# An eighth V slot in the gather ring of a streaming encoder, with the space for it taken from three work buffers

## The chip, the core and the metric

The kernel runs on one core of a Trainium2 chip: TensorE (PE) multiplies matrices, VectorE (DVE), ScalarE (ACT) and GpSimd (POOL) work beside it, and SyncE (SP) issues plain transfers. Sixteen DMA engines carry all transfers of the core between HBM and the on-chip memory. The metric is the device time of the whole kernel in microseconds (us).

## What is computed

One step of an encoder layer for 1024 prompt rows and 32 sample rows of width 1024: an input projection, an mLSTM and a sliding-window attention on its halves, an output projection, and then PEER, a layer that fetches single experts by index. PEER does most of the work here. Cut to what matters:

```
def block(xb):                                    # peer, 128 rows at a time
    q = (xb @ w_q).reshape(TB, PEER_HEADS, PEER_KEY_DIM)
    s1 = jnp.einsum('thd,nd->thn', q[..., :PEER_HALF], sub_keys_1)
    s2 = jnp.einsum('thd,nd->thn', q[..., PEER_HALF:], sub_keys_2)
    t1, i1 = lax.top_k(s1, PEER_TOPK)
    t2, i2 = lax.top_k(s2, PEER_TOPK)
    cand = (t1[..., :, None] + t2[..., None, :]).reshape(...)
    cidx = (i1[..., :, None] * N_KEYS + i2[..., None, :]).reshape(...)
    top, sel = lax.top_k(cand, PEER_TOPK)
    idx = jnp.take_along_axis(cidx, sel, axis=-1)
    g = jax.nn.softmax(top.astype(jnp.float32), axis=-1)
    u = jnp.take(expert_u, idx, axis=0)
    a = jax.nn.gelu(jnp.einsum('thkd,td->thk', u, xb), approximate=False)
    ve = jnp.take(expert_v, idx, axis=0)
    return jnp.einsum('thk,thkd->td', g * a, ve)
```

There are 8 heads with 16 picks each, so every row fetches 128 rows of `peer_u` and 128 of `peer_v`, 4 KB each. At the end each row is normalised once more (`rmsnorm(x, norm_final_w)`).

## The kernel before

**Tiles and groups.** The rows are cut into 9 tiles of up to 128 rows. For PEER, 32 rows of a tile times 4 heads fill the 128 partitions: that is a group. Two groups (a pair) cover the 8 heads of 32 rows; there are 66 groups. A group has 16 steps, one for each pick. In a step one U tile (128 rows of `peer_u`) and one V tile (128 rows of `peer_v`), each 512 KB, are gathered with an indirect DMA.

**The ring.** The gathers land in `ring`, which has `NU` = 5 slots for U and `NV` = 7 for V. GpSimd issues all gathers in one fixed order, U of the next group and V of this one in turn (lines 583 and 594). Before a U gather it waits until VectorE has finished with the slot (`u_free`), before a V gather until TensorE has (`v_free`, line 590). The first V gathers wait for nothing, except that slots 5 and 6 hold staging pieces (`po`) of the first projection, whose stores must have ended (`proj_out`, line 593).

**A step on each engine.** VectorE multiplies the U tile with the spread rows `h2p` and sums (line 1255), giving one dot product for each partition. ScalarE turns a group's dots into gelu weights (line 822). VectorE makes the weight matrices `wk` of a group from them (`weigh`, line 1210). TensorE multiplies the V tile with its weight matrix into `acc` (line 1651). VectorE is one group ahead of TensorE. At the end of a pair TensorE moves the right half, which stands in other partitions, over: ScalarE copies it to `part` (`gather_parts`, line 833) and TensorE brings it back (line 1606). TensorE also spreads the rows of the next pair into `h2p` (`spread_rows`, line 1597), once VectorE has its last dot of the pair; VectorE waits for that before the next pair.

**Top-k.** VectorE picks the 16 experts of a group three groups ahead, in 11 stages (`topk`), one stage behind each of the steps 0 to 10. Stages 8 and 9 turn the flat position of each pick into two key indices: the position's high and low four bits are compared with 0 to 15 (a one-hot row, line 1190), multiplied with the key indices `i2f` (line 1193) and summed (line 1195). Stage 10 writes `idx`, from which GpSimd gathers. Both indices are done side by side in `co`, whose first half is also `cand`, the candidates.

**All else** is laid between the steps by tables of step numbers (`PE_AT`, `ACT_AT`, `DVE_AT` with `slot_of`): the projections, mLSTM, attention, queries and key scores of the next tiles. Each engine runs its own list in the order written. In attention four matrix products with `ident` write the window mask `wmask` into the scores (line 1481) before the keys are added. At a tile's end ScalarE takes the squares of the finished rows into `part` (`square_rows`, line 844).

## Time and profile before

| | before |
|---|---|
| median of 3 runs | 3442.43 us (3436.01 to 3443.79) |
| the profiled execution | 3454.89 us |
| its span, first to last instruction | 3453.2 us |
| mean granted TensorE clock | 0.810 of full speed |
| busy: TensorE / VectorE / GpSimd / ScalarE | 76% / 61% / 58% / 16% |
| gathers (software queue) | 1107.43 MB of 1197.01 MB in all |

Busy shares are means over the whole kernel. A row of the waits view says which engine, at which tile and line, stood idle until what, with the total, the number of times and the longest. In the timeline a row gives start, duration, engine, line and operation, how many instructions were merged, and in brackets the idle time of the engine before it and what ended it. "issue" means that nothing in the profile explains the gap, and "remote" that the releaser could not be named.

### The profile page before, as it was taken

Reading aid. Unit: us, or ns where it says so; the run is one execution under the profiler, and the core shown is the slowest. Engines: PE = TensorE matmul, PEld = TensorE weight load, DVE = VectorE, ACT = ScalarE, POOL = GpSimd, SP = SyncE. Lnnn points to the kernel's source line nnn. Section 1 sums busy time; section 2 is a strip of 40 time slices with the busy share of each in tenths; the row PEclk is TensorE's granted clock in tenths of the full one; section 3 lists DMA queues with packets and bytes.
Section 4 is the critical chain, followed back from the end, with each engine's and each line's share of the span. In section 5 each row is a group of like instructions: output and inputs, shape, how many; then the busy total and the mean of one; then the engine's idle time right before and its main releaser. Section 6 shows DMA issues by size and latency. Waiting matters only on the chain.

```text
span 3453.2 us, 33371 instructions
## 1 busy us (share of the span) xinstructions
PE 2628.1 (76%) x10989; PEld 1019.2 (30%) x10989; DVE 2102.2 (61%) x5216; ACT 552.1 (16%) x1066; POOL 1992.9 (58%) x2128
## 2 busy tenths in 40 slices
PE   8987787678667898988776877688676776676666
PEld 4552342224222532223332232124222331121101
DVE  1256657666676566657567656666666666666653
ACT  2211111111121131112012111111111111111001
POOL 0026556655656566655556666666665666666665
PEclk9997896889678899988888886688777886677656
DMA  6479899999999999999899999999999999999998
GB/s 226 154 277 374 306 338 366 353 346 344 367 338 359 343 401 408 394 395 353 327 340 337 363 358 370 353 360 336 371 363 345 360 352 370 348 352 357 376 359 327
DMA packets 348917, 1197.01 MB, mean 347 GB/s; under 512 B 37760, under 2 KB 54408, under 8 KB 346952
## 3 DMA queue, kind: packets, MB, share of 16 engines
q0 software_dynamic: 304128, 1107.43, 85.2%
q1 hardware_dynamic: 44616, 87.45, 6.9%
q8 instruction: 86, 1.41, 0.2%
q14 instruction: 87, 0.71, 0.1%
HBM read 1180.69 MB, written 14.15 MB: 346 GB/s over the span
## 4 chain that ended last, share of the span: by engine, by line
PE 35%; DVE 14%; issue 13%; DMA 12%; POOL 10%; another core or an unknown queue 9%; DVEq 5%; ACT 1%; ACTq 0%; SPq 0%; POOLq 0%
PE acc L1651 11%; PE mx L1543 8%; DVE ring L1255 7%; DMA ring<-in_peer_v_dram,idx 6%; DMA ring<-in_peer_u_dram,idx 5%; POOL ring L594 5%; POOL ring L583 5%; PE mx L1359 3%; DVEq L1146 3%; PE mx L1525 3%; PE acc L1335 2%; PE mx L1554 2%; PE acc L1322 1%; PE h2p L1597 1%
## 5 line engine op out<-in xcount | busy, mean ns | idle before, releaser
L1651 PE MATMUL acc<-ring,wk 128*32 128x512 f32 x4224 | 1387.3, 747 | 594.7 <-DMA ring<-in_peer_v_dram,idx 336.3
L1255 DVE SCALAR_TENSOR_TENSOR ring<-ring,h2p 128x1024 f32<-128x1024 f32 x1056 | 1275.4, 1215 | 654.3 <-DMA ring<-in_peer_u_dram,idx 362.4
L583 POOL DMA_INDIRECT ring<-in_peer_u_dram,idx x1056 | 995.6, 943 | 798.3 <-DVE ring L1255 318.4
L594 POOL DMA_INDIRECT ring<-in_peer_v_dram,idx x1056 | 995.2, 942 | 646.0 <-issue 280.9
L1651 PEld LDWEIGHTS acc<-ring,wk 128*32 128x32 f32 x4224 | 218.9, 122 | 1499.7 <-DMA ring<-in_peer_v_dram,idx 719.0
L1543 PE MATMUL mx<-reg,weights 128*128 128x128 f32 x1792 | 258.7, 296 | 50.9 <-issue 50.7
L1543 PEld LDWEIGHTS mx<-reg,weights 128*128 128x128 f32 x1792 | 230.8, 205 | 156.9 <-issue 156.8
L1525 PE MATMUL mx<-weights,reg 128*128 128x512 f32 (+1 forms) x256 | 132.9, 641 | 2.7 <-issue 2.7
L1359 PE MATMUL mx<-weights 128*128 128x512 f32 (+1 forms) x288 | 125.3, 578 | 0.7 <-issue 0.7
L822 ACT ACTIVATE gl<-dots 128x16 f32<-128x16 f32 x66 | 14.2, 216 | 628.0 <-issue 469.6
L1597 PE MATMUL h2p<-ch,ident 32*32 32x512 f32 x528 | 82.7, 719 | 22.2 <-DVEq L1258 12.7
L782 ACT COPY pj<-mx 128x512 f32<-128x512 f32 x32 | 18.8, 586 | 459.0 <-remote 245.3
L1554 PE MATMUL mx<-kT,pj 128*32 128x128 f32 x1040 | 71.0, 314 | 27.3 <-issue 18.7
L1255 DVE DVE_READ_ACCUMULATOR ring<-ring,h2p 128x1 f32 x1056 | 86.9, 82 | 0.0
L822 ACT ACT_TABLE_LOAD x66 | 84.7, 1283 | 5.9 <-issue 0.4
L816 ACT ACT_TABLE_LOAD x61 | 78.3, 1283 | 29.6 <-DVEq L1211 15.3
L1359 PEld LDWEIGHTS mx<-weights 128*128 128x128 f32 x288 | 53.0, 194 | 75.0 <-issue 72.6
L1525 PEld LDWEIGHTS mx<-weights,reg 128*128 128x128 f32 (+1 forms) x256 | 44.0, 190 | 95.2 <-issue 94.3
L1554 PEld LDWEIGHTS mx<-kT,pj 128*32 128x32 f32 x1040 | 50.2, 124 | 57.7 <-issue 46.1
L1218 DVE TENSOR_TENSOR xt<-xt,acc 32x1024 f32<-32x1024 f32 x33 | 40.1, 1216 | 33.8 <-PE acc L1606 23.1
L1193 DVE TENSOR_TENSOR co<-co,i2f 128x256 f32<-128x256 f32 x132 | 50.6, 424 | 9.0 <-issue 3.2
L1190 DVE TENSOR_TENSOR co<-ij,iota 128x256 f32<-128x256 uint32 x132 | 50.2, 422 | 9.4 <-issue 4.9
(304 smaller groups left out, 2367.1 us busy)
## 6 DMA issues: line engine op xcount, KB each, us to landing
ring<-in_peer_u_dram,idx POOLq DMA_INDIRECT x1056
ring<-in_peer_v_dram,idx POOLq DMA_INDIRECT x1056
weights<-in_peer_w_q_dram SPq DMA_DIRECT2D x7, 2048.0 KB
weights<-in_w_in_dram SPq DMA_DIRECT2D x5, 2048.0 KB, 18.1
weights<-in_w_in_dram SPq DMA_DIRECT2D x10, 1024.0 KB
ring<-in_peer_w_q_dram SPq DMA_DIRECT2D x8, 1024.0 KB, 5.6
xt<-in_x_prompt_dram SPq DMA_DIRECT2D x8, 512.0 KB
ring<-in_w_out_dram SPq DMA_DIRECT2D x2, 2048.0 KB, 14.0
```

The lines of the kernel that those rows point to most:

```text
L583: pool.indirect_dma_start(ring[:, n % NU, :], None, u_d, bass.IndirectOffsetOnAxis(ap=idx[:, g % 4, k:k + 1], axis=0)).then_inc(u_in[n % N ...
L594: pool.indirect_dma_start(ring[:, NU + n % NV, :], None, v_d, bass.IndirectOffsetOnAxis(ap=idx[:, g % 4, k:k + 1], axis=0)).then_inc(v_in[ ...
L816: S.activation(ew[:, :], top[:, g % 3, :], ACT.Exp, bias=ntop[:, g % 3:g % 3 + 1], accum_out=ez[:, 0:1])
L822: S.activation(gl[:, :], dots[:, g % 2, :], ACT.Gelu)
L1146: dve.drain()
L1255: V.scalar_tensor_tensor(ring[:, n % NU, :], ring[:, n % NU, :], 1.0, h2p[:, :], ALU.mult, ALU.mult, accum_out=dots[:, (g + 1) % 2, k:k + ...
L1359: last = T.matmul(bank, hT1_again[i][:, 4 * half + k, :], wpiece[(2 * p + half) % 3][:, k, 0:w], start=half + k == 0, stop=half == 1 and k ...
L1525: last = T.matmul(mx[0:n, 2 + half, :], t8[:, k, 0:n], w, start=k == 0, stop=k == DC - 1)
L1543: last = T.matmul(mx[:, i // 4, i % 4 * P:i % 4 * P + n], w, t8[:, k, 0:n], start=k == 0, stop=k == DC - 1)
L1554: last = T.matmul(mx[q:q + SUB, i, col:col + NK], qT[:, c, i * SUB:(i + 1) * SUB], kT[:, c % 2, :], start=True, stop=True)
L1597: last = T.matmul(h2p[j * SUB:(j + 1) * SUB, cols], ident[r, r], ch[m % 2][r, cols], start=True, stop=True)
L1651: last = T.matmul(acc[j:j + SUB, cols], wk[:, g % 2, n % TOPK, :], ring[:, NU + n % NV, cols], start=g % 2 == 0 and n % TOPK == 0, stop=g ...
```

## The change

Every [P, 1024] slot takes 4 KB of each partition. The change adds a slot for V and takes its space from three other buffers:

- `NV` goes from 7 to 8. The staging pieces move with it: piece 5 goes from the right half of `part` to V slot 5, pieces 6 and 7 lie in slot 6, pieces 8 and 9 in slot 7, and the first nine projection units use piece 8 in place of 5. The first V gathers wait for the stores of those pieces accordingly.
- `co` (two halves) becomes `cand` alone. Stage 8 makes the one-hot rows of the first index and multiplies them; stage 9 sums them, then compares, multiplies and sums for the second index in the same buffer.
- `part` is 512 columns wide. It holds the moved right half, and the squares at a tile's end are taken in two halves, with the first half's sum going in as a bias.
- `wmask` has one column for each 64 keys, and the matrix product reads each of them 64 times.

```diff
-NV = 7
+NV = 8
...
-UNIT_PO = [n % 6 for n in range(BEHIND)] + [4, 5, 6, 7, 8, 9, 4, 5, 6]
+UNIT_PO = [(0, 1, 2, 3, 4, 8)[n % 6] for n in range(BEHIND)] + [4, 5, 6, 7, 8, 9, 4, 5, 6]
...
-        co = sb("co", [P, 2, TOPK, TOPK])
-        cand = co[:, 0]
+        cand = sb("cand", [P, TOPK, TOPK])[:, :, :]
...
-        part = sb("part", [P, D])
-        yr = sb("yr", [P, 3])
+        part = sb("part", [P, 512])
+        yr = sb("yr", [P, 5])
...
-        wmask = sb("wmask", [P, 2 * P])
+        wmask = sb("wmask", [P, 4])
...
-        po += [a[:, h * 512:h * 512 + 512] for a in (part, ring[:, NU + 5, :], ring[:, NU + 6, :]) for h in range(2)]
+        po += [part[:, :], ring[:, NU + 5, 0:512]] + [a[:, h * 512:h * 512 + 512] for a in (ring[:, NU + 6, :], ring[:, NU + 7, :]) for h in range(2)]
...
-            pool.memset(wmask[:, 0:WIN], -BIG)
-            pool.memset(wmask[0:CHUNK, WIN + CHUNK:], -BIG)
+            pool.memset(wmask[:, 0:2], -BIG)
+            pool.memset(wmask[0:CHUNK, 3:4], -BIG)
...
-                elif n >= NV - 2:
-                    for b in (6, 7) if n == NV - 2 else (8, 9):
+                elif n >= NV - 3:
+                    for b in {NV - 3: (5,), NV - 2: (6, 7), NV - 1: (8, 9)}[n]:
...
-                S.copy(part[other, 512:], acc[other, 512:])
+                S.copy(part[other, :], acc[other, 512:])
...
-                    S.activation(part[0:n, :], xt[m % 2][0:n, :], ACT.Square, accum_out=yr[0:n, 0:1])
+                    S.activation(part[0:n, :], xt[m % 2][0:n, 0:512], ACT.Square, scale=D ** -0.5, accum_out=yr[0:n, 0:1])
                     act.drain()
-                    S.activation(yr[0:n, 1:2], yr[0:n, 0:1], ACT.Sqrt, scale=1.0 / D, bias=epsc[0:n, 0:1])
+                    S.activation(yr[0:n, 3:4], yr[0:n, 0:1], ACT.Identity, bias=epsc[0:n, 0:1])
+                    S.activation(part[0:n, :], xt[m % 2][0:n, 512:], ACT.Square, scale=D ** -0.5, accum_out=yr[0:n, 4:5])
+                    act.drain()
+                    S.activation(yr[0:n, 1:2], yr[0:n, 4:5], ACT.Sqrt, bias=yr[0:n, 3:4])
...
-                    for a in range(2):
-                        V.tensor_tensor(co[:, a], bc(ij[:, a, :].unsqueeze(2), P, TOPK, TOPK), bc(iota[:, :].unsqueeze(1), P, TOPK, TOPK), ALU.is_equal)
+                    V.tensor_tensor(cand, bc(ij[:, 0, :].unsqueeze(2), P, TOPK, TOPK), bc(iota[:, :].unsqueeze(1), P, TOPK, TOPK), ALU.is_equal)
+                    dve.drain()
+                    V.tensor_tensor(cand, cand, bc(i2f[:, 0, :].unsqueeze(1), P, TOPK, TOPK), ALU.mult)
                 elif stage == 9:
-                    for a in range(2):
-                        V.tensor_tensor(co[:, a], co[:, a], bc(i2f[:, a, :].unsqueeze(1), P, TOPK, TOPK), ALU.mult)
-                    dve.drain()
-                    V.tensor_reduce(r2[:, :, :], co[:, :, :, :], AX.X, ALU.add)
+                    V.tensor_reduce(r2[:, 0, :], cand, AX.X, ALU.add)
+                    dve.drain()
+                    V.tensor_tensor(cand, bc(ij[:, 1, :].unsqueeze(2), P, TOPK, TOPK), bc(iota[:, :].unsqueeze(1), P, TOPK, TOPK), ALU.is_equal)
+                    dve.drain()
+                    V.tensor_tensor(cand, cand, bc(i2f[:, 1, :].unsqueeze(1), P, TOPK, TOPK), ALU.mult)
+                    dve.drain()
+                    V.tensor_reduce(r2[:, 1, :], cand, AX.X, ALU.add)
...
-                            T.matmul(mx[:, b, :].rearrange("p (h s) -> p h s", h=2), ident[:, :], wmask[:, :].unsqueeze(1).broadcast_to([P, 2, 2 * P]), start=True, stop=False)
+                            T.matmul(mx[:, b, :].rearrange("p (h c s) -> p h c s", h=2, c=4), ident[:, :], wmask[:, :].unsqueeze(1).unsqueeze(3).broadcast_to([P, 2, 4, CHUNK]), start=True, stop=False)
```

On VectorE, stages 8 and 9 of a group between the dot products (`ring,dots`) of steps 8, 9 and 10, first as they stand before (`ij` holds the picks' high and low bits, `r` the two sums):

```order
L1255 SCALAR_TENSOR_TENSOR ring,dots<-ring,h2p 128x1024
L1186 TENSOR_SCALAR ij<-sel 128x16
L1187 TENSOR_SCALAR ij<-sel 128x16
L1190 TENSOR_TENSOR co<-ij,iota 128x256 x2
L1255 SCALAR_TENSOR_TENSOR ring,dots<-ring,h2p 128x1024
L1193 TENSOR_TENSOR co<-co,i2f 128x256 x2
L1195 TENSOR_REDUCE r<-co 128x32
L1255 SCALAR_TENSOR_TENSOR ring,dots<-ring,h2p 128x1024
```

and as they stand now:

```order
L1261 SCALAR_TENSOR_TENSOR ring,dots<-ring,h2p 128x1024
L1188 TENSOR_SCALAR ij<-sel 128x16
L1189 TENSOR_SCALAR ij<-sel 128x16
L1191 TENSOR_TENSOR cand<-ij,iota 128x256
L1193 TENSOR_TENSOR cand<-cand,i2f 128x256
L1261 SCALAR_TENSOR_TENSOR ring,dots<-ring,h2p 128x1024
L1195 TENSOR_REDUCE r<-cand 128x16
L1197 TENSOR_TENSOR cand<-ij,iota 128x256
L1199 TENSOR_TENSOR cand<-cand,i2f 128x256
L1201 TENSOR_REDUCE r<-cand 128x16
L1261 SCALAR_TENSOR_TENSOR ring,dots<-ring,h2p 128x1024
```

One product moved ahead of the step 9 dot product, and one comparison moved behind it.

On GpSimd, the first V gathers that wait for a store or a slot, before:

```order
L594 DMA ring<-in_peer_v_dram,idx 128x1024
L583 DMA ring<-in_peer_u_dram,idx 128x1024 [waits u_free]
L594 DMA ring<-in_peer_v_dram,idx 128x1024 [waits proj_out7,proj_out6]
L583 DMA ring<-in_peer_u_dram,idx 128x1024 [waits u_free]
L594 DMA ring<-in_peer_v_dram,idx 128x1024 [waits proj_out9,proj_out8]
L583 DMA ring<-in_peer_u_dram,idx 128x1024 [waits u_free]
L594 DMA ring<-in_peer_v_dram,idx 128x1024 [waits v_free]
```

and now:

```order
L593 DMA ring<-in_peer_v_dram,idx 128x1024
L582 DMA ring<-in_peer_u_dram,idx 128x1024 [waits u_free]
L593 DMA ring<-in_peer_v_dram,idx 128x1024 [waits proj_out5]
L582 DMA ring<-in_peer_u_dram,idx 128x1024 [waits u_free]
L593 DMA ring<-in_peer_v_dram,idx 128x1024 [waits proj_out7,proj_out6]
L582 DMA ring<-in_peer_u_dram,idx 128x1024 [waits u_free]
L593 DMA ring<-in_peer_v_dram,idx 128x1024 [waits proj_out9,proj_out8]
L582 DMA ring<-in_peer_u_dram,idx 128x1024 [waits u_free]
L593 DMA ring<-in_peer_v_dram,idx 128x1024 [waits v_free]
```

The order of the gathers is the same; the waits for the stores stand one V gather later, and the first wait for a used slot too.

## Rows read from the trace of the kernel before

**Rows 1.** Windows view: busy us (instructions) by engine, granted clock, DMA share, GB/s.
```profile
1300.00:1500.00 200.00, 183.64 (x585) 58.68 (x585) 122.26 (x301) 30.50 (x47) 124.45 (x133) 0.97 1.02 401
2100.00:2300.00 200.00, 144.26 (x492) 49.25 (x493) 139.94 (x357) 30.99 (x69) 126.68 (x135) 0.73 0.94 353
```
**Rows 2.** Costliest groups: count | busy us, mean ns of one | idle before, releasers.
```profile
L594 POOL DMA_INDIRECT ring<-in_peer_v_dram,idx x1056 | 995.2, 942 | 646.0 <-issue 280.9
```
**Rows 3.** Waits view of the whole span: us in total, times, longest.
```profile
DVE ring L1255 <- DMA ring<-in_peer_u_dram,idx: 362.4, 243, 6.3
...
POOL ring L583 <- DVE ring L1255: 318.4, 161, 11.1
...
POOL ring L594 <- remote: 197.9, 93, 4.5
POOL ring L583 <- DVEq L1198: 187.9, 1, 187.9
...
POOL ring L594 <- PE acc L1651: 147.0, 122, 5.1
...
POOL ring L594 <- DMA proj_scratch<-ring: 19.0, 1, 19.0
```
**Rows 4.** Timeline: gathers on GpSimd and dot products on VectorE, at three places.
```profile
456.68 0.93 POOL L594 DMA_INDIRECT ring<-in_peer_v_dram,idx  x1 [4.04 <-remote]
...
2819.07 0.94 POOL L583 DMA_INDIRECT ring<-in_peer_u_dram,idx  x1 [0.30 <-issue]
2821.03 0.94 POOL L594 DMA_INDIRECT ring<-in_peer_v_dram,idx  x1 [1.02 <-PE acc L1651]
2821.47 1.22 DVE L1255 SCALAR_TENSOR_TENSOR ring<-ring,h2p 128x1024 f32<-128x1024 f32 x1 [0.78 <-DMA ring<-in_peer_u_dram,idx]
...
3407.59 0.93 POOL L594 DMA_INDIRECT ring<-in_peer_v_dram,idx  x1 [4.47 <-remote]
```
**Rows 5.** Timeline: VectorE's first dot product of a pair, boundary near 2390 us.
```profile
2389.57 1.22 DVE L1255 SCALAR_TENSOR_TENSOR ring<-ring,h2p 128x1024 f32<-128x1024 f32 x1 [9.52 <-PE h2p L1597]
```
**Rows 6.** Timeline: TensorE's spreading and VectorE's next dot product, boundary near 2570 us.
```profile
2566.87 1.91 PE L1597 MATMUL h2p<-ch,ident 32*32 32x512 f32 x15 [0.36 <-issue]
...
2576.70 1.22 DVE L1255 SCALAR_TENSOR_TENSOR ring<-ring,h2p 128x1024 f32<-128x1024 f32 x1 [3.92 <-remote]
```
**Rows 7.** Stages 8 and 9 of the first group in the timeline, and one group row.
```profile
188.02 0.76 DVE L1190 TENSOR_TENSOR co<-ij,iota 128x256 f32<-128x256 uint32 x2 [0.37 <-issue]
188.85 0.76 DVE L1193 TENSOR_TENSOR co<-co,i2f 128x256 f32<-128x256 f32 x2
189.69 0.69 DVE L1195 TENSOR_REDUCE r<-co 128x32 f32<-128x512 f32 x1
...
L1190 DVE TENSOR_TENSOR co<-ij,iota 128x256 f32<-128x256 uint32 x132 | 50.2, 422 | 9.4 <-issue 4.9
```
**Rows 8.** Timeline of SyncE's issues: the stores of the last two projection units.
```profile
253.18 0.32 SPq L424 DMA_DIRECT2D proj_scratch<-part  x1
259.09 0.32 SPq L424 DMA_DIRECT2D proj_scratch<-ring  x1
```
**Rows 9.** ScalarE: two groups by shape, and the squares at the end of the kernel.
```profile
L742 ACT ACTIVATE reg<-pj 128x512 f32<-128x512 f32 x8 | 5.0, 630 | 39.2 <-DVEq L1066 22.9 <-issue 16.1
L844 ACT ACTIVATE part<-xt 128x1024 f32<-128x1024 f32 x8 | 8.5, 1057 | 102.1 <-issue 59.0 <-DVEq L1219 43.1
...
3448.59 0.18 ACT L844 ACTIVATION_READ_ACCUMULATOR part<-xt 32x1 f32 x1
3448.85 0.29 ACT L846 ACTIVATE yr<-yr,epsc 32x1 f32<-32x1 f32 x1
```
**Rows 10.** TensorE groups by shape: the mask products, their weight loads, and spreading loads.
```profile
L1481 PE MATMUL mx<-wmask,ident 128*128 128x512 f32 x64 | 30.3, 617 | 0.0
L1583 PEld LDWEIGHTS mx<-ffw,ident 8*128 8x128 f32 x128 | 24.3, 277 | 15.8 <-issue 15.6
L1481 PEld LDWEIGHTS mx<-wmask,ident 128*128 128x128 f32 x64 | 12.0, 197 | 20.0 <-issue 20.0
```

More of the change, by code:

```diff
@@ L514, in _ @@
                 store_unit(n)
-            for b in range(7):
+            for b in range(10):
                 sp.wait_ge(proj_out[b], stored(b, BEHIND + 3))
@@ L830, in gather_parts @@
                 if q == 0:
-                    for b in (4, 5):
+                    for b in (4,):
                         act.wait_ge(proj_out[b], stored(b, len(UNITS)))
-                S.copy(part[other, 512:], acc[other, 512:])
+                S.copy(part[other, :], acc[other, 512:])
                 act.drain().then_inc(part_ready, 1)
@@ L1109, in mix @@
                     if m == 0:
-                        V.memset(wmask[:, 0:WIN], 0.0)
+                        V.memset(wmask[:, 0:2], 0.0)
                         dve.drain()
-                        V.memset(wmask[CHUNK:P, 0:CHUNK], -BIG)
+                        V.memset(wmask[CHUNK:P, 0:1], -BIG)
                     dve.drain().then_inc(cat_ready, 1)
@@ L1605, in gather_parts @@
                 pe.wait_ge(part_ready, q + 1)
-                T.matmul(acc[r, 512:], ident[other, other], part[other, 512:], start=True, stop=True).then_inc(sub_ready, 1)
+                T.matmul(acc[r, 512:], ident[other, other], part[other, :], start=True, stop=True).then_inc(sub_ready, 1)
             def begin_parts(q):
```

## The prediction

> **What bounds the kernel now.** I read the profile from the resource most used to the waits that join the engines. First the windows: over 2100 to 2300 us the core's DMA engines are busy 0.94 of the time at 353 GB/s, yet over 1300 to 1500 us they moved 401 GB/s [rows 1]. The reader is to see a memory side that is nearly full but has given more elsewhere, so part of the time between gathers comes from the engines. Second, GpSimd: one gather issue takes 942 ns [rows 2] and the next follows 0.30 us behind [rows 4], so a gather every 1.24 us is its own pace, 2.6 ms for the 2112 gathers. The rest are waits for slots and for the first index.
>
> Third, who waits for whom [rows 3]. GpSimd waits 318.4 us in 161 places for a U slot that VectorE frees, and 197.9 + 147.0 = 344.9 us in 215 places before a V gather. A V gather waits for nothing but its slot, so both rows are TensorE being behind, also where the releaser is called remote. Each of these gaps contains the ordinary 0.30 us, so 344.9 - 215 x 0.30 = 280 us of V waiting is real. This is the most that an eighth slot can remove. VectorE in turn waits 362.4 us in 243 places for U rows to land.
>
> Fourth, the timeline, because a wait of GpSimd costs only where an engine then starves. I went through its 181 V gathers that waited over 0.1 us beyond their 0.30 (305 us in all, since some stand under other releasers than those two) and looked at what came next. In 71 places (101 us) the next event was another V wait: TensorE was slower than the gathers for a stretch, and one more slot only shifts the queue. In 42 places (77 us) it was a U wait. In 10 nothing followed soon. In 58 places (106 us) VectorE next started a row late for want of a U landing; the first is at 456.68 us, the last at 3407.59 us, and and at 2821.03 and 2821.47 us a V wait and a late VectorE step stand side by side [rows 4]. Taking in each of the 58 the smaller of the wait and the starvation gives 76 us, 1.3 us a place.
>
> Fifth, the exchange every 32 steps: TensorE spreads new rows into h2p (line 1597), for which it needs VectorE's last dot product of the pair, and VectorE needs h2p to go on. Two sorts of boundary show. At 2389.57 us VectorE had stood idle for 9.52 us and was released by h2p: TensorE came to it late [rows 5]. At 2566.87 us TensorE was there at once after VectorE's last row, and VectorE went on later, at 2576.70 us, for reasons of its own work [rows 6]. Of the 32 boundaries 16 are of each sort. In a pair that TensorE ends late, GpSimd's V waits are the echo of TensorE's load and a further slot gives nothing. A gain can come only in the other 16.
>
> **The eighth slot.** GpSimd can be one V gather further ahead of TensorE. The lead is credited once and is not renewed before TensorE has caught up, so I credit each of the 16 VectorE-late pairs with one starvation of the mean size: 16 x 1.3 = 21 us. Bounds: nothing (every wait turns into a U wait, as 42 places already do), and 51 us, the part of the 76 us that lies in those pairs. Gather order and the alternation of U and V are unchanged.
>
> **The start of the ring.** Before, the sixth V gather stands behind the last unit's store, issued at 259.09 us, and waits 19.0 us for it [rows 3, 8]. Now it needs only the unit stored at 253.18 us, and the seventh takes over the wait. That lets one V and one U gather out earlier, at most 2 x 1.24 = 2.5 us. I take 1.
>
> **One-hot rows for one index at a time.** Before, the two comparisons overlap (0.76 us for two), so do the two products (0.76), and one reduction takes 0.69, with about 0.08 between dependent steps [rows 7]. Alone a 128x256 comparison takes 422 ns [rows 7]. After, everything depends on what stands before it. The stage with the comparisons goes from 0.76 to 0.42 + 0.08 + 0.42 = 0.92, that is +0.16. The next goes from 0.76 + 0.08 + 0.69 = 1.53 to four instructions of 0.42 (a 256-wide reduction taken like a 256-wide comparison, between half of 0.69 and that) and three gaps, 1.92, that is +0.39. Together +0.55 us a group, 36 us over 66 groups. Queued behind are the next dot product, the index store and so, three groups ahead, the gathers; those have slack. The dot product has none where rows are already there: in the first group of a VectorE-late pair, and in part of the second, where it otherwise starves and hides it. 16 x 0.55 + half as much again = 13 us. Ends: 4, and 36 with no cover at all. Ahead of the very first gather nothing hides it (the 187.9 us wait [rows 3]): +0.55.
>
> The Trainium skill, page "VectorE: DVE Perf Modes", section "The TRN2 errata", says that many small tiles pay a fixed bubble each, and gives an fp32 tensor-tensor operation as (N+151)/0.96 ns. Worked out as an estimate, that makes one extra instruction of 0.15 us a group and 10 us over the kernel; it has no term for the lost overlap that the 0.76 us pairs show. By it the sum would be some 9 us lower.
>
> **The half-width buffer.** The final squares become two of 512 columns; 630 ns is the nearest row, against 1057 for 1024 [rows 9]: +0.20. A second accumulator read of 0.18 and a small bias operation like the root of 0.29 [rows 9] join it: +0.67 in all. Eight of the nine times ScalarE hides it, being mostly idle; the last is on the tail: +0.7. The copy of the moved half is as before.
>
> **The mask of four columns.** 64 matrix products of 617 ns now read one word 64 times over [rows 10]. The nearest zero-step read is a weight load that spreads a column, 277 ns against 197 for a plain one [rows 10]; the same ratio would add 0.41 x 30.3 = 12 us on TensorE, about half of it in pairs that TensorE ends. The other end is nothing, and I take it, since the same number of columns streams through. The smaller fills of the mask save tenths at the start.
>
> **Sum.** -21 - 1 + 13 + 0.55 + 0.7 = -8 us. The profiled execution took 3454.9 us (span 3453.2), so it would become 3447; it lies 12 us over the 3442.4 us median, and against the median the forecast is 3435 us.
>
> **The rivals.**
> (a) Full release. TensorE is less often late than its recorded stretches suggest, and most of the 51 us and some of the other waits come back: 3442 - 51 + 14 = about 3405. For it: V waiting is the second largest wait of GpSimd. Against: 178 of the 305 us are followed by another slot wait. Chance 0.16.
> (b) Displacement. V waits fall by a third or more and U waits rise by as much; VectorE and the pair exchange set the pace as before. The gain is 0 to 14 us and eats only the added work: 3437 to 3449. For it: GpSimd takes U and V in turn, and U has only five slots. Chance 0.27.
> (c) Memory is the bound. The windows show 0.94 busy at 353 GB/s, so a deeper queue only lands later: no gain, 3442 + 14 = 3456 if VectorE's price holds, 3446 if cover is good. Against: 401 GB/s in another stretch [rows 1]. Chance 0.08.
> The Trainium skill, page "DMA: Bandwidth & Descriptors", section on one software-queue DMA, puts data movement at 436 GB/s beside a fixed cost of about 2 us. By it a gather moves in 1.20 us, memory is no bound at all, and this rival falls; rows 1 show 401 GB/s at full business, less than that.
> (d) VectorE becomes the bound, the case on the other side: two thirds of the added 36 us show because the chain of six dependent instructions falls in steps where VectorE has landed rows waiting, and the slot gives little. 3442 + 24 - 5 = 3461. It decides once VectorE is the later engine at clearly more than 16 of the 32 boundaries. Chance 0.12.
> The change not doing what it says, V gathers still waiting seven behind, can't be in this code: slot and wait both follow NV.
>
> **How the numbers follow.** The forecast case, a credit in part of the late pairs less the added work, spans 3424 to 3441 and has 0.37; about a fifth of it lies within 0.2% of before. About 0.2%, 7 us, is what a measurement of this kernel can tell from no change. Faster by more: 0.30 of the forecast, all of (a), 0.03 of (b): 0.49. Within: 0.07 of the forecast, 0.20 of (b), 0.03 of (c): 0.30. Slower: 0.04 of (b), 0.05 of (c), all of (d): 0.21. The range reaches down into (a) and up to (c) with the mask's few microseconds: 3408 to 3457, leaving out the lower half of (a) and (d).
>
> **What would show it.** After the change V waits of GpSimd should be near 200 us in place of 345, in fewer places, and U waits up from 318 towards 400; VectorE's waits for U landings down by some 20 to 60 us; VectorE busier by 15 to 36 us, with the two stages' rows at 0.9 and 1.9 us; the mask products still 617 ns at a like clock; the number of boundaries at which h2p releases VectorE about the same. U waits unchanged with V waits gone would be (a); V waits gone and VectorE's landing waits unchanged would be (b) or (c), told apart by the DMA share. The forecast is wrong if the 16 VectorE-late pairs are not where time is saved, or if one added dependent step costs more than 0.08 us of gap.

## The result, and the profile after

| | before | after |
|---|---|---|
| median | 3439.22 us (3428.56 to 3443.79, 4 runs) | 3482.64 us (3472.77 to 3495.62, 4 runs) |
| ratio | | 1.0133 (1.0088 to 1.0178) |
| the profiled execution | 3454.89 us | 3488.16 us |
| its span | 3453.2 us | 3486.4 us |
| mean granted TensorE clock | 0.810 | 0.809 |
| busy: TensorE / VectorE / GpSimd / ScalarE | 76% / 61% / 58% / 16% | 76% / 61% / 57% / 16% |

The change made the kernel 1.3% slower here, some 43 us. It was forecast 7 us faster, and the range ended at 3457. The first thing to read is what the slot did to GpSimd, the waits view of the kernel after (us in total, times, longest), where [rows 3] had 318.4 us for a U slot and 197.9 + 147.0 us for a V slot:

```profile
POOL ring L582 <- DVE ring L1261: 410.8, 192, 9.8
...
POOL ring L582 <- DVEq L1204: 191.7, 1, 191.7
POOL ring L593 <- remote: 179.9, 76, 4.9
POOL ring L593 <- PE acc L1657: 103.8, 109, 4.1
POOL ring L593 <- DMA proj_scratch<-ring: 18.2, 1, 18.2
```

Waiting for V slots fell from 344.9 to 283.7 us and from 215 to 185 places, and waiting for U slots rose by 92.4 us. GpSimd's whole idle time, whoever ended it, moves alike: 646.0 to 589.6 us ahead of the V gathers, 798.3 to 886.3 us ahead of the U gathers. So the slot is in use, and what GpSimd no longer waits for TensorE it waits, and more, for VectorE. VectorE's side of the same execution (waits view, then the group view: count | busy us, mean ns | idle before):

```profile
DVE ring L1261 <- DMA ring<-in_peer_u_dram,idx: 297.3, 199, 6.4
...
DVE ez L1210 <- ACTq L822: 83.4, 19, 14.5
```

```profile
L1210 DVE RECIPROCAL ez<-ez 128x1 f32<-128x1 f32 x66 | 10.6, 161 | 103.6 <-ACTq L822 83.4 <-issue 20.1
```

It waits less for U rows to land (362.4 before), and its whole idle time ahead of the dot products falls from 654.3 to 561.6 us, so memory is not what holds it up. It waits longer at the reciprocal of `ez`, the first thing that it does behind ScalarE's gelu. In the kernel before this group reads:

```profile
L1204 DVE RECIPROCAL ez<-ez 128x1 f32<-128x1 f32 x66 | 10.6, 161 | 55.3 <-ACTq L823 31.0 <-issue 24.3
```

The added work looks as it was meant to. Timeline of the kernel after (start, us, and in brackets the idle time before), stages 8 and 9 of the first group, to be read against [rows 7]; then two groups:

```profile
190.84 0.43 DVE L1191 TENSOR_TENSOR cand<-ij,iota 128x256 f32<-128x256 uint32 x1 [0.37 <-issue]
191.34 0.42 DVE L1193 TENSOR_TENSOR cand<-cand,i2f 128x256 f32<-128x256 f32 x1
191.84 0.42 DVE L1195 TENSOR_REDUCE r<-cand 128x16 f32<-128x256 f32 x1
192.34 0.43 DVE L1197 TENSOR_TENSOR cand<-ij,iota 128x256 f32<-128x256 uint32 x1
192.84 0.43 DVE L1199 TENSOR_TENSOR cand<-cand,i2f 128x256 f32<-128x256 f32 x1
193.34 0.42 DVE L1201 TENSOR_REDUCE r<-cand 128x16 f32<-128x256 f32 x1
```

```profile
L1191 DVE TENSOR_TENSOR cand<-ij,iota 128x256 f32<-128x256 uint32 x66 | 28.1, 426 | 9.7 <-issue 5.2
...
L1201 DVE TENSOR_REDUCE r<-cand 128x16 f32<-128x256 f32 x66 | 27.7, 420 | 6.0 <-issue 1.3
```

One dependent step follows the last by 0.50 us, 0.42 of work and 0.08 between. Six of them take 5 x 0.50 + 0.42 = 2.92 us, where [rows 7] took 189.69 + 0.69 - 188.02 = 2.36. On ScalarE and TensorE, by shape, the halves of the squares and the mask products:

```profile
L843 ACT ACTIVATE part<-xt 128x512 f32<-128x512 f32 x8 | 5.0, 630 | 96.9 <-issue 49.5 <-DVEq L1225 47.4
...
L846 ACT ACTIVATE part<-xt 128x512 f32<-128x512 f32 x8 | 4.9, 615 | 0.0
```

```profile
L1487 PE MATMUL mx<-wmask,ident 128*128 128x512 f32 x64 | 32.1, 647 | 3.3 <-issue 3.3
```

The windows of [rows 1] after (busy us and instructions by engine, clock, DMA share, GB/s):

```profile
1300.00:1500.00 200.00, 178.93 (x556) 57.00 (x555) 118.09 (x286) 31.03 (x51) 118.95 (x127) 0.91 0.98 382
...
2100.00:2300.00 200.00, 138.66 (x467) 47.37 (x463) 135.19 (x347) 36.38 (x77) 123.75 (x132) 0.70 0.93 352
```

Neither stretch moves more than before. The first moves 382 GB/s in place of 401, with 127 instructions on GpSimd, nearly all of them gathers, in place of 133; the second 352 in place of 353. TensorE, VectorE and GpSimd are busy for less of the 200 us in both, ScalarE for more (36.38 us in place of 30.99 in the second). As the kernel runs later by then, the two pairs of windows don't hold quite the same work.

### The profile page after: what moved, and what is told of

Same layout as the page of the kernel before. It is cut to its first block, busy times and chain, and to the rows that moved or that the text cites. A ratio compares the mean times of both kernels' runs of the same rounds, so it can differ in the third digit from the quotient of the medians.

```text
span 3486.4 us, 33673 instructions
## 1 busy us (share of the span) xinstructions
PE 2638.1 (76%) x10989; PEld 1027.8 (29%) x10989; DVE 2119.7 (61%) x5282; ACT 556.2 (16%) x1093; POOL 1994.1 (57%) x2128
## 3 DMA queue, kind: packets, MB, share of 16 engines
q8 instruction: 86, 1.41, 0.2%
## 4 chain that ended last, share of the span: by engine, by line
PE 31%; issue 18%; DVE 15%; another core or an unknown queue 12%; DMA 9%; POOL 8%; DVEq 5%; ACT 2%; ACTq 0%; SPq 0%; POOLq 0%
PE acc L1657 10%; DVE ring L1261 6%; PE mx L1549 6%; DMA ring<-in_peer_v_dram,idx 4%; POOL ring L593 4%; POOL ring L582 4%; DMA ring<-in_peer_u_dram,idx 4%; DVEq L1148 3%; PE mx L1365 3%; PE mx L1531 2%; PE acc L1341 2%; PE mx L1560 1%; PE acc L1328 1%; PE h2p L1603 1%
## 5 line engine op out<-in xcount | busy, mean ns | idle before, releaser
L1261 DVE SCALAR_TENSOR_TENSOR ring<-ring,h2p 128x1024 f32<-128x1024 f32 x1056 | 1273.1, 1215 | 561.6 <-DMA ring<-in_peer_u_dram,idx 297.3
L582 POOL DMA_INDIRECT ring<-in_peer_u_dram,idx x1056 | 996.3, 943 | 886.3 <-DVE ring L1261 410.8
L593 POOL DMA_INDIRECT ring<-in_peer_v_dram,idx x1056 | 996.1, 943 | 589.6 <-issue 286.6
L1531 PE MATMUL mx<-weights,reg 128*128 128x512 f32 (+1 forms) x256 | 134.7, 651 | 4.2 <-issue 4.0
L1603 PE MATMUL h2p<-ch,ident 32*32 32x512 f32 x528 | 90.5, 734 | 35.4 <-issue 24.8
L1261 DVE DVE_READ_ACCUMULATOR ring<-ring,h2p 128x1 f32 x1056 | 86.9, 82 | 0.0
L1210 DVE RECIPROCAL ez<-ez 128x1 f32<-128x1 f32 x66 | 10.6, 161 | 103.6 <-ACTq L822 83.4
L1365 PE MATMUL mx<-weights,reg 128*128 128x512 f32 (+1 forms) x96 | 45.0, 616 | 11.0 <-DMA weights<-in_w_in_dram 9.3
```

What stands on the lines that cost most here:

```text
L582: pool.indirect_dma_start(ring[:, n % NU, :], None, u_d, bass.IndirectOffsetOnAxis(ap=idx[:, g % 4, k:k + 1], axis=0)).then_inc(u_in[n % N ...
L593: pool.indirect_dma_start(ring[:, NU + n % NV, :], None, v_d, bass.IndirectOffsetOnAxis(ap=idx[:, g % 4, k:k + 1], axis=0)).then_inc(v_in[ ...
L1261: V.scalar_tensor_tensor(ring[:, n % NU, :], ring[:, n % NU, :], 1.0, h2p[:, :], ALU.mult, ALU.mult, accum_out=dots[:, (g + 1) % 2, k:k + ...
L1365: last = T.matmul(bank, hT1_again[i][:, 4 * half + k, :], wpiece[(2 * p + half) % 3][:, k, 0:w], start=half + k == 0, stop=half == 1 and k ...
L1531: last = T.matmul(mx[0:n, 2 + half, :], t8[:, k, 0:n], w, start=k == 0, stop=k == DC - 1)
L1603: last = T.matmul(h2p[j * SUB:(j + 1) * SUB, cols], ident[r, r], ch[m % 2][r, cols], start=True, stop=True)
```

## Experiments: what the cuts cost

The change has two sides, the slot and the space for it. First each cut alone on the kernel before, and all of them with V gathers kept to seven of the eight slots. These four shared a chip, on which the kernel before took 3466.94 us (35 runs).

One-hot rows for one index at a time, on the kernel before (the two stages as in the diff ahead):

```diff
-        co = sb("co", [P, 2, TOPK, TOPK])
-        cand = co[:, 0]
+        cand = sb("cand", [P, TOPK, TOPK])[:, :, :]
...
```

> The kernel before with the one-hot rows made for one index at a time and nothing else. Theory S: 1.000 to 1.004, since 36 us more on VectorE lie mostly beside other work. Theory D: 1.008 to 1.014.

Measured: 3464.1 us, 0.9997 (0.9983 to 1.0011).

The mask of four columns, on the kernel before:

```diff
-        wmask = sb("wmask", [P, 2 * P])
+        wmask = sb("wmask", [P, 4])
...
```

> The kernel before with the mask of four columns alone. Theory S and D: 0.999 to 1.001, 617 ns for a mask product at a like clock. Theory M (a repeated read is slower): 1.002 to 1.005 and products of 700 to 900 ns.

Measured: 3463.87 us, 0.9999 (0.9983 to 1.0016).

The squares in two halves, on the kernel before:

```diff
-                    S.activation(part[0:n, :], xt[m % 2][0:n, :], ACT.Square, accum_out=yr[0:n, 0:1])
+                    S.activation(part[0:n, 0:512], xt[m % 2][0:n, 0:512], ACT.Square, scale=D ** -0.5, accum_out=yr[0:n, 0:1])
...
```

> The kernel before with the final squares taken in two halves; the buffer keeps its size. All theories: 1.000 to 1.001, 0.7 us more at the tail. Above 1.002 would mean that ScalarE's order matters more than its 16% busy share says.

Measured: 3469.75 us, 1.0004 (0.9988 to 1.002).

All three and the moved staging, with seven slots in turn:

```diff
 NV = 8
+NR = 7
...
-                    pool.wait_ge(v_free, n - NV + 1)
+                    pool.wait_ge(v_free, n - NR + 1)
...
-                pool.indirect_dma_start(ring[:, NU + n % NV, :], None, v_d,
+                pool.indirect_dma_start(ring[:, NU + n % NR, :], None, v_d,
```

> All three cuts and the moved staging, but V gathers use seven of the eight slots; the eighth holds only staging pieces. Theory S (the slot in use costs the time: V gathers get further ahead in the one gather queue and TensorE may lag further, while the cuts cost little): ratio to before 0.998 to 1.004. Theory D (the dependent one-hot chain costs it, the slot gives about nothing): 1.010 to 1.016, as with the whole change. If the slot helps and the cuts cost more than the whole change, above 1.016.

Measured: 3464.37 us, 0.9995 (0.998 to 1.0011). So the cuts cost nothing that can be measured, 0.1% at the most, and the loss has to come from the slot being used (taken together with the changed kernel on another chip; the two stand side by side further down).

## Experiments: the slot, the lead and the chip

Next the changed kernel again, beside three ways to use thirteen slots. In `wait7` all eight V slots are in turn, but a gather starts when the product seven steps back is done:

```diff
-                if n >= NV:
-                    pool.wait_ge(v_free, n - NV + 1)
-                elif n >= NV - 3:
+                if NV - 3 <= n < NV:
                     for b in {NV - 3: (5,), NV - 2: (6, 7), NV - 1: (8, 9)}[n]:
                         pool.wait_ge(proj_out[b], stored(b, len(UNITS)))
+                lead = NV - 1
+                if n >= lead:
+                    pool.wait_ge(v_free, n - lead + 1)
```

`wait6` has `lead = NV - 2`. `u6v7` gives the added slot to U:

```diff
-NU = 5
-NV = 8
+NU = 6
+NV = 7
...
```

The staging pieces stay where they are in the changed kernel.

> The changed kernel as it is, for a second time, beside the kernel before and the three next kernels on one chip. Both theories of this group: ratio to the kernel before 1.009 to 1.018, some 3500 us where the kernel before takes 3455. If it comes out at 1.000 the loss belonged to the first chip and not to the slot.

> The changed kernel with its eight V slots in turn, but GpSimd starts the gather of V n only when the V product of step n - 7 is done (before and in the kernel before: seven ahead; in the changed kernel: eight). Theory L (lead: letting V gathers run one further ahead is what costs): ratio 1.000 +- 0.002 to the kernel before, 45 us under the changed kernel. Theory R (rotation: eight slots in turn, which fall on the same slot every 8 steps and so on the same in each group of 16, cost by where they lie): ratio of the changed kernel, 1.013.

> As the one ahead, with the gather of V n started when the V product of step n - 6 is done. Theory L as a straight line: less lead is better still, ratio 0.99 to 1.00. Theory L with a best lead at seven, which the kernel before had found: slower than it, 1.005 to 1.02, with GpSimd's waits for V slots longer than 342 us. Theory R: 1.013 or more.

> The changed kernel with the thirteen slots shared out as six for U and seven for V in place of five and eight. Theory L in the form that a V row ahead takes the queue's place of the U row which VectorE needs next: the extra slot on U's side helps, ratio 0.985 to 0.998, and VectorE's waits for U landings fall under 297 us. In the form that more rows in flight only crowd the queue, whichever table they are from: 1.005 to 1.015. Theory R: 1.000, since V is back at seven slots in turn.

They came to run on a chip where the kernel before takes 3129.84 us (29 runs), a tenth less than on the two so far. I call the two sorts below by this time; whether it is a property of the chip or of the occasion comes at the end, and "slower chip" below means no more than a chip on such an occasion. Measured there: the changed kernel 3133.27 us, 1.001 (0.9999 to 1.002). `wait7` 1.0029 (1.0017 to 1.004). `wait6` 1.0048 (1.0031 to 1.0065). `u6v7` 0.9989 (0.9979 to 0.9998). Here lead is of some use, about 0.2% a step, and the loss of 1.3% is gone. The expectation that it would repeat was wrong, and the other three, written for the slower chips, miss too: `wait7` is a little above its 1.000 +- 0.002, `wait6` a little under its 1.005, and `u6v7` gains less than the least forecast for it (0.998).

The next four were to be read on either kind of chip:

> The changed kernel for a third time. It was 1.0133 (1.0088 to 1.0178) on a chip where the kernel before takes 3439 us and 1.001 (0.9999 to 1.002) on one where it takes 3130 us. Theory C (the loss belongs to chips whose traces show engines standing still with nothing to wait for): 1.008 to 1.018 where the kernel before takes 3440 to 3470 us, 1.001 where it takes 3130 us. Theory X (four runs were too few, and the slot costs or gains next to nothing anywhere): 0.999 to 1.004 on either kind of chip.

> Eight V slots in turn, gathers seven ahead, again. It was 1.0029 where the changed kernel was 1.001. Theory L (lead) on a chip of 3440 to 3470 us: 1.000 to 1.004, well under the changed kernel, since the lead is what costs there. Theory R (rotation over eight): within 0.002 of the changed kernel, or above it.

> The four column mask, the one-hot rows of one index at a time and the half buffers, with V gathers in seven of the eight slots in turn. It was 0.9995 on a chip of 3467 us. Both theories: 0.998 to 1.002. On a chip of 3130 us, where memory moves 382 GB/s, it tells whether the 0.3% of the eight in turn with seven ahead comes with the cuts (then 1.002 to 1.004 here) or with the rotation (then 0.998 to 1.001).

> Six U slots and seven V slots, again. It was 0.9989 (0.9979 to 0.9998). If the added slot is worth more on U's side: 0.995 to 0.999 on either kind of chip, and under the changed kernel by 0.2% or more. If any thirteenth slot in use costs on a chip of 3440 to 3470 us (Theory C for both sides): 1.008 or more there.

It was a third chip like the last, 3131.13 us before (35 runs). The changed kernel 1.001 (0.9996 to 1.0024), `wait7` 1.0017 (1.0003 to 1.0031), seven in turn with the cuts 1.0014 (1.0004 to 1.0024), `u6v7` 0.999 (0.9978 to 1.0002). So on these chips the cuts cost 0.1%, and eight in turn with seven ahead cost no more than seven in turn within the intervals: no effect of the order of the slots shows. Nor does one of the lead on this chip, 1.001 against 1.0017 and 1.0014.

What differs there is best seen in rows. The waits view of the changed kernel in this execution, and of the one with seven slots in turn:

```profile
POOL ring L582 <- DVE ring L1261: 348.6, 337, 6.9
...
POOL ring L593 <- PE acc L1657: 57.8, 171, 1.6
```

```profile
POOL ring L583 <- DVE ring L1262: 318.0, 296, 7.3
...
POOL ring L594 <- PE acc L1658: 86.1, 189, 2.6
```

Again 28 us of V waits go and 31 us of U waits come, and the time stays: this is rival (b), displacement, alone. There is no row with the releaser `remote` here, which in the kernel before had 197.9 of the 344.9 us of V waits. And in the changed kernel on this chip TensorE's query products wait once for nothing that the profile shows, and the reciprocal stands 25.6 us idle:

```profile
PE mx L1549 <- issue: 1.1, 1, 1.1
```

```profile
L1210 DVE RECIPROCAL ez<-ez 128x1 f32<-128x1 f32 x66 | 10.6, 160 | 25.6 <-ACTq L822 25.2 <-issue 0.4
```

In the execution of the first comparison the row for the same products is this (waits view of the kernel after), and the timeline shows what such a wait looks like, in a series of query products that follow one another:

```profile
PE mx L1549 <- issue: 68.3, 61, 2.5
```

```profile
783.47 0.94 PE L1549 MATMUL mx<-reg,weights 128*128 128x128 f32 x6
786.53 0.27 PE L1549 MATMUL mx<-reg,weights 128*128 128x128 f32 x1 [2.13 <-issue]
788.65 0.27 PE L1549 MATMUL mx<-reg,weights 128*128 128x128 f32 x1 [1.85 <-issue]
790.77 0.37 PE L1549 MATMUL mx<-reg,weights 128*128 128x128 f32 x1 [1.85 <-issue]
793.56 0.37 PE L1549 MATMUL mx<-reg,weights 128*128 128x128 f32 x1 [2.42 <-issue]
794.97 0.37 PE L1549 MATMUL mx<-reg,weights 128*128 128x128 f32 x1 [1.03 <-issue]
```

Six matmuls take 0.94 us together, and the next five end at 795.34 us, 10.9 us later. Nothing in the program stands between them but their weight loads. VectorE has such gaps too. Counting those of over 600 ns ahead of an instruction that carries no wait, on TensorE matmuls and on VectorE (us in total):

| kernel, chip by the time of the kernel before | V ahead | TensorE | VectorE | ratio |
|---|---|---|---|---|
| before, 3439 | 7 | 85.9 | 57.6 | 1 |
| mask / squares / one-hot, 3467 | 7 | 86.9 / 96.2 / 99.2 | 63.1 / 64.0 / 73.9 | 0.9999 / 1.0004 / 0.9997 |
| cuts, seven in turn, 3467 | 7 | 87.4 | 52.4 | 0.9995 |
| after, 3439 | 8 | 121.7 | 87.1 | 1.0133 |
| changed kernel, 3130 and 3131 | 8 | 0 | 0 | 1.001 |

All six executions on the slower chips have these gaps (and the four that follow), none of the ten on the faster ones has. Their spacing is regular. The five starts in the timeline above lie 2.12, 2.12, 2.79 and 1.41 us apart, which is 3, 3, 4 and 2 steps of 0.70 to 0.71 us. In that execution every two counted gaps in a row that end less than 4 us apart (49 pairs on TensorE, 17 on VectorE) are within 0.06 us of a multiple of 0.706 us apart, and in the nine other executions on slower chips 393 of 404 pairs are. What sets this step the profile doesn't say.

Three more things differ. A packet of the gathers takes 154.7 ns on average in the kernel before and 148.1 ns in the changed kernel at 3130 us. The mean granted clock is 0.80 to 0.81 in the slower executions and 0.83 to 0.84 in the faster, and TensorE is busy for 2603 to 2667 us in place of 2508 to 2537 with the same matmuls. And the traces of the slower ones lack records: of the 3279 semaphore increments by the program's engines they hold 2184 to 2326, those of the faster ones all, and of the increments by landings 14000 to 15000, where the faster ones hold 36300. Which of these brings which I can't tell from these traces.

The lacking records bear on the readings. Where the increment that ended a wait is not on record, the view calls the wait "issue" or "remote", or gives it to another releaser. The row `remote` above, and a part of the "issue" rows, are such waits. The table and the idle times of whole groups don't depend on the increments: they go by the instructions' starts and ends, and of these the changed kernel has the same number, 33673, on either sort of chip.

The comparison that was missing is the slot and the lead together on a slower chip:

> The changed kernel again, on whichever chip it falls. Theory C: 1.008 to 1.018 where the kernel before takes 3430 to 3470 us, and there TensorE and VectorE show gaps of over 600 ns ahead of instructions that wait for nothing (90 and 49 of them in the first trace), 1.001 where it takes 3130 us (no such gap). Theory X: 0.999 to 1.004 whatever the chip.

> Eight V slots in turn, seven ahead. If the chip is one of 3430 to 3470 us and the changed kernel is at 1.008 or more: Theory L 1.000 to 1.004, Theory R within 0.002 of the changed kernel. If the changed kernel is at 0.999 to 1.004 there: 1.001 to 1.004, as on the chip of 3130 us.

> Six U slots and seven V slots. On a chip of 3430 to 3470 us: 0.993 to 0.999 if a slot more on U's side also covers the gaps of the engines there, 1.005 or more if any thirteenth slot in use costs there. On a chip of 3130 us 0.999 as before.

This time it was one of 3469.48 us (17 runs). The changed kernel took 3507.91 us, 1.0117 (1.0091 to 1.0144), so the loss of the first comparison was no accident. `wait7` took 3466.38 us, 0.9988 (0.9972 to 1.0005). The two kernels differ in one constant on GpSimd, and 41.5 us lie between them: it is the lead of one V gather more that costs, and not the cuts, the rotation or the place of the slot. `u6v7` took 3429.38 us, 0.9892 (0.9866 to 0.9918): the same thirteenth slot on U's side brings 40 us. Both came out better than the best that was expected of them, 1.000 and 0.993. The waits view of `wait7` and then of `u6v7` on that chip:

```profile
POOL ring L582 <- DVE ring L1262: 313.5, 169, 9.9
...
POOL ring L594 <- remote: 200.8, 97, 4.9
...
POOL ring L594 <- PE acc L1658: 153.9, 127, 5.1
```

```profile
POOL ring L593 <- remote: 228.7, 109, 4.6
...
POOL ring L593 <- PE acc L1657: 197.0, 134, 5.3
POOL ring L582 <- DVE ring L1261: 187.2, 137, 9.0
```

In `wait7` the sum of V waits is 354.7 us and that of U waits 313.5, in `u6v7` 425.7 and 187.2. The faster kernel waits more for V slots. The wait that I had called the most that the slot can remove is thus not what the kernel pays for; the wait for U slots, ahead of a row that VectorE will want, may be nearer to it, which is argued and not shown. The gaps without a reason are 86.7 and 75.4 us (TensorE, VectorE) in `wait7`, 123.9 and 88.9 in the changed kernel, and 66.4 and 55.0 in `u6v7`.

TensorE's own work differs too. From `wait7` to the changed kernel the span grows by 39.1 us (3466.1 to 3505.2), of which TensorE is busy for 13.7 (2653.6 to 2667.3) and idle for 25.4, while its gaps without a reason grow by 37.2. From `wait7` to `u6v7` the span falls by 48.8 us, and that is all busy time: 2653.6 to 2603.4, at a granted clock of 0.802 and 0.811, with 812.5 and 814.0 us idle. So a different clock goes with the gain of the U slot, and which of the two brings the other isn't shown.

## Experiments: by which way the lead costs

The reciprocal's row gave the next theory. Idle time ahead of it: 52 to 65 us in the seven executions with seven ahead on the slower chips, 104 and 100 with eight. Here `wait7` and the changed kernel on the chip of 3469 us:

```profile
L1211 DVE RECIPROCAL ez<-ez 128x1 f32<-128x1 f32 x66 | 10.6, 161 | 65.1 <-ACTq L823 40.8 <-issue 24.3
```

```profile
L1210 DVE RECIPROCAL ez<-ez 128x1 f32<-128x1 f32 x66 | 10.6, 161 | 100.2 <-ACTq L822 65.1 <-issue 35.0
```

The timeline of ScalarE and VectorE at group 29 of the changed kernel shows one case:

```profile
1719.29 0.59 ACT L781 COPY pj<-mx 128x512 f32<-128x512 f32 x1 [24.28 <-PE mx L1549]
...
1721.26 0.22 ACT L821 ACTIVATE gl<-dots 128x16 f32<-128x16 f32 x1
```

```profile
1705.60 1.22 DVE L1261 SCALAR_TENSOR_TENSOR ring<-ring,h2p 128x1024 f32<-128x1024 f32 x1 [0.95 <-DMA ring<-in_peer_u_dram,idx]
```

VectorE ends the group's last dot product at 1706.82 us. The gelu starts at 1721.26, since ScalarE works in order and stood at the copy of a query product that TensorE reached only behind more V steps. In `wait7` the gelu of this group starts 11.6 us after the last dot product, in the changed kernel 14.4. Fifteen groups are of this kind: their gelus start 116.8 us after their last dot products in total in the changed kernel and 73.3 in `wait7`, those of the other fifty-one 10.9 and 8.7. So I moved these fifteen ahead of the copy that stands before each, in the changed kernel:

```diff
+GELU_AT = {5: 12, 11: 12, 12: 11, 19: 11, 20: 13, 21: 13, 22: 11, 23: 13, 25: 13, 26: 11, 29: 13, 30: 12, 35: 12, 43: 12, 51: 12}
...
-                    if k == TOPK - 1 and g + 1 < GROUPS:
+                    if k == GELU_AT.get(g + 1, TOPK - 1) and g + 1 < GROUPS:
                         gelu(g + 1)
```

> The changed kernel, in which ScalarE runs the gelu of 15 of the 66 groups (5, 11, 12, 19 to 23, 25, 26, 29, 30, 35, 43, 51) two to four slots earlier in its list, just ahead of the copy of a TensorE product that stood before it. Nothing is left out. In the traces of two chips of 3440 to 3470 us VectorE stood idle 104 and 100 us ahead of the reciprocal that follows the gelu with eight slots of lead, and 52 to 65 us in six kernels with seven; in those 15 groups the gelu began up to 15 us after the group's last dot product. Theory G (TensorE runs one more V step behind, so a copy that waits for it holds the gelu back, and VectorE stops): on such a chip that idle time falls to 60 us or less and the ratio from 1.012 or 1.013 to 0.998 to 1.005. Rival K (the lead costs in another way, such as the gaps of TensorE with nothing to wait for, 123 us against 87, and the late gelu only goes with it): the idle time falls but the ratio stays at 1.008 or more. On a chip of 3130 us both: 0.999 to 1.002, since the idle time is 25 us there with seven or eight.

Measured on a chip of 3464.81 us (11 runs): 3488.59 us, 1.0085 (1.0059 to 1.011). The gelu of group 29 now starts 0.1 us after the last dot product, and of the idle time ahead of the reciprocal 20 us are left:

```profile
1699.28 0.21 ACT L822 ACTIVATE gl<-dots 128x16 f32<-128x16 f32 x1 [14.70 <-issue]
1710.19 0.59 ACT L782 COPY pj<-mx 128x512 f32<-128x512 f32 x1 [10.70 <-PE mx L1550]
```

```profile
L1211 DVE RECIPROCAL ez<-ez 128x1 f32<-128x1 f32 x66 | 10.6, 161 | 20.3 <-issue 11.4 <-ACTq L823 9.0
```

80 us less of VectorE's idle time brought some 0.3 to 0.5%, 11 to 17 us, and the intervals of 1.0085 and of 1.0117 overlap, so even that is not certain. Theory G had forecast 1.005 at the most and doesn't carry the loss; Rival K had forecast 1.008 or more and stands. VectorE gives a part back at the exchange of h2p: its wait for that is 129.8 us here, 93.4 us in the changed kernel of the run before. The gaps without a reason are 125.3 us on TensorE and 81.7 us on VectorE, as in the other two executions with eight ahead.

The last two were to tell whether the move is worth as much with seven ahead, and what it adds to `u6v7`:

> Eight V slots in turn, gathers seven ahead, with the 15 gelus moved forward as in gelu_v8 (1.0085 of the kernel before). Without the move it was 0.9988. On a chip of 3440 to 3510 us: if the late gelu is a part of what the eighth of lead costs, the move is worth less here than the 0.3 to 0.5% that it brought with eight, since the idle time ahead of the reciprocal is 65 us here and 100 there: 0.996 to 0.999. If the move is worth as much here (0.994 to 0.995), the late gelu costs both alike and has no part in the difference. On a chip of 3130 us 1.001 to 1.003.

> Six U slots and seven V slots (0.9892 on a chip of 3469 us, 0.9989 and 0.999 on two of 3130 us) with the 15 gelus moved forward. The idle time ahead of the reciprocal was 54 us without the move. On a chip of 3440 to 3510 us 0.984 to 0.989 if both add up, 0.989 to 0.992 if the move brings nothing on top; on a chip of 3130 us 0.998 to 1.000.

They fell on a chip of 3130.49 us: 1.0023 (1.0013 to 1.0033) and 0.9994 (0.9986 to 1.0003), as without the move. There the idle time ahead of the reciprocal is 14 us in place of 25, and the time doesn't follow. They say nothing about the slower chips, so how much of the lead's price is the late gelu stays open.

## Why the prediction was wrong, point by point

**The slot's term failed, in sign.** The prediction credited "16 x 1.3 = 21 us". The lead alone costs 41.5 us on a chip like the one of the forecast (1.0117 against 0.9988). On the other kind it brings at most some 6 us: 1.001 against 1.0029 on one chip, 1.001 against 1.0017 with eight in turn and 1.0014 with seven on the other, where the intervals overlap. The step that failed is the fourth reading: a V wait followed by a starved VectorE was taken as the cause of that starvation, and its bounds as "nothing" and 51 us, with no end on the side of a loss. It also read landing waits off a trace that holds 14036 of some 36300 landing increments. The intermediate signs were right: U waits toward 400 (410.8), VectorE's landing waits down by 20 to 60 (by 65, a little past it). V waits fell to 284 in place of some 200. An engine that waited less for rows still ended later, because other waits took their place: the reciprocal's (+48 us), and the gaps without a reason (+36 us on TensorE, +30 on VectorE).

**What costs is only in part known.** Shown: the cost is in the lead of the V gathers, is there on both chips of 3440 to 3470 us that ran the changed kernel and on neither of the two of 3130 us, and goes with later gelus and more unexplained gaps. Shown as well: taking the late gelus away leaves 0.85%. Not shown: that the gaps are the rest. They rise and fall with the time (122 to 125 us on TensorE with eight ahead, 86 to 99 with seven, 66 in `u6v7`), but no run changed them alone, and what they are the profile doesn't say. TensorE's busy time, 13.7 of the 39.1 us between the spans of `wait7` and the changed kernel, wasn't set apart either.

**The one-hot term was right in its size a group and wrong in its price.** +0.55 us a group was forecast, 2.92 - 2.36 = 0.56 us is seen in the first group, and VectorE is busy 17.5 us longer (2119.7 against 2102.2). But of the 36 us no 13 came to the end: alone the edit measured 0.9997, with an upper end of +0.11%, 4 us, which is the lower bound that the prediction named. VectorE's idle time takes it up: 1337.0 us with the edit alone, beside 1370.1 and 1367.1 in the mask and the squares kernel on the same chip.

**Squares and mask at nothing were right**, 1.0004 and 0.9999. The halves took 630 and 615 ns where 630 was forecast. The mask product was to stay at 617 ns at a like clock; its mean is 647 here, 635 in the squares kernel with the old mask and 658 in the one with the new. The means differ by how many of the 64 fell into stretches of low clock. By the view of the tile `wmask`, the shortest, median and longest of the 64 take 592, 592 and 1222 ns in the kernel before, 592, 592 and 1222 in the mask kernel and 592, 592 and 1219 in the kernel after. So the zero-step read costs nothing, and the bound of 12 us stood on a ratio that doesn't carry over from weight loads.

**The start of the ring**: the one long wait ahead of a V gather is 18.2 us in place of 19.0; whether the 1 us credited for it came can't be told beside the rest. The first gather waited 191.7 us in place of 187.9, of which the one-hot chain explains 0.56; it was 191.4 in the mask kernel, which has no such chain. At the exchange of h2p VectorE was held up in 15 places in place of 12, about the same, as said (68.1 us in place of 73.2).

**The rivals.** (b), displacement, at 0.27, is what happens on the chips of 3130 us. On the chip of the forecast none of the four holds: (a) forecast a large gain, (c) put the loss on memory, and (d), the only one on the slower side, took VectorE's added work as the cause, with 3461. Left out was a slower kernel through the slot itself. The other thing left out is that the "issue" rows were passed over. The kernel before showed 159.6 us of them ahead of TensorE's V products alone (waits view):

```profile
PE acc L1651 <- issue: 159.6, 145, 7.7
```

A part of these are waits whose end is not on record. But 85.9 us in all on TensorE are gaps ahead of instructions that wait for nothing, and the kernel's time is a tenth above what the same program needs where there are none. The third reading, that 280 us of V waiting are real, holds for that chip only: at 3131 us the V gathers' waits for TensorE come to 86.1 us with seven in turn, so most of what the slot was to work on is not there.

## What to carry to other kernels

One more buffer is not free of risk where one in-order queue serves two consumers. It lets one consumer fall further behind the other, and what waits for both can come later: here the gelus behind a copy did, though moving them brought back 0.3 to 0.5% at the most of the 1.2 to 1.3%. Before adding a buffer, ask on which side the wait costs: the same slot brought 1.1% on U's side and lost 1.2% on V's, though V's waits were the longer. And test the size and the lead apart, with the wait on a constant of its own.

`u6v7` beats both kernels on both kinds of chip, clearly on the one (0.9892) and by 0.1% on the other, which the interval of the second comparison hardly tells from no change.

## What was not expected of the hardware

- The same program, the kernel before, takes 3130 us on some chips and 3439 to 3469 us on others. The changed kernel moves 382 GB/s over its span on a faster one and 343 on a slower.
- On the slower chips TensorE stands still for up to 3.2 us and VectorE for up to 4.7 us ahead of instructions that wait for nothing, several in a row, some 140 us in the kernel before on the two engines together. They tend to come back in the same places of the program: of 90 such gaps on TensorE in the changed kernel and 97 in its second execution on such a chip, 22 stand ahead of the very same matmul, and on VectorE 25 of 49 and 50 ahead of the very same instruction. Gaps close together end 0.70 to 0.71 us apart, or a multiple of it. On the faster chips there is none.
- The traces with these gaps also lack a third of their semaphore increments. Whether the two have one cause no run here shows. The execution whose trace is shown is not a slow one among its neighbours: with seven slots in turn it took 3472.6 us, the others 3451 to 3473.
- A matmul that reads each word of its moving operand 64 times over takes as long as one that reads 256 different words twice, 592 ns (median of 64 in the kernels after and before).
- The sort need not belong to the chip: `gelu_v8` and the last two kernels ran under the same chip number, the kernel before taking 3464.81 us beside the first and 3130.49 us beside the others. Either the number repeats from machine to machine, or something outside the program comes and goes. Between the repeated runs of one comparison it didn't change.
- An edit can cost 1.2% on one occasion and 0.1% on the next, so a ratio belongs to the chip and the hour at which it was measured.
